# Decode state updates of a hybrid decoder step, head by head in 32- and 64-column tiles of the array

## The chip, the cores and the metric

The kernel runs on one core of one Trainium2 chip. The metric is the device time of one execution in microseconds; before the change it is 2575.82 us, the median of 3 runs (2574.97 to 2575.86).

## The reference

One inference step of a two-layer decoder trunk: 1024 prompt tokens and 8 decode sequences of 4 new tokens each (32 rows), model width 1024. Each layer projects x, runs a retention group (4 heads, keys of 32, values of 64), an HGRN2 group (4 heads, keys and values of 64) and a sliding-window attention group, joins them in one output projection, and ends with a feed-forward block; both halves end with a residual addition and a layer norm. The part that the change touches is the update of the recurrent states of the 8 decode sequences, over chunks of L = 4 tokens:

```python
# retention, per sequence n and head h: (32 keys) x (64 values)
kdec = k * jnp.exp((L - 1.0 - idx)[:, None] * lg[None, :])[None, :, :, None]
s = jnp.exp(L * lg)[None, :, None, None] * s0 + jnp.einsum('nshk,nshv->nhkv', kdec, v)
# HGRN2, per sequence and head: (64 keys) x (64 values)
bl = b[:, -1]
s = jnp.exp(bl)[..., None] * s0 + jnp.einsum('nshk,nshv->nhkv', k * jnp.exp(bl[:, None] - b), v)
```

Only products of a head's keys with the same head's values are part of the states. The outputs are the two token streams, the new states and the window caches.

## The kernel before, in words

TensorE (PE), VectorE (DVE), ScalarE (ACT), GpSimd (POOL) and the DMA queue of SyncE (SP) each run a program written out by hand, in order; `Steps` counts named events on a semaphore, and `wait_ge(S.sem, S.at(name, n))` waits for one. A layer has four stages: `project` (input projection of the first tiles), `mix` (the three head groups, tile by tile, with units of the late input projection and of the output projection in between, placed by the table `PLACES`), `attend_out` (the rest of the output projection with residual and norm) and `feed`.

`mix` goes through steps 0 to 9; in each, tile `f` is in its front part and the tile before it, `h`, in its heads part. Tiles 0 to 7 are the prompt, tile 8 the 32 decode rows. Step 9 has no dense unit; it holds only the heads part of the decode tile. There PE runs, in this order: transposes and level products, `decode_heads_out` with the partial outputs of all sequences from the old states (L1644, L1651), the **retention state products** (L1657), the joined output (L1661, L1664, L1668); then `decode_states` with the **HGRN2 state products** (L1678), and the transposes of the merged heads (L1351 from `heads_transposed`). An fp32 product is two instructions of PE in the trace.

The state products work on whole rows of the array. The 8 retention products take `kdm[0:32, b, :]`, the keys of all four heads with the rows of other sequences set to zero by POOL (L3487), as 32 x 128 weights and stream 256 value columns, so all 16 pairs of head and head come out, in banks 4 to 7; only the four diagonal ones are used. The 16 HGRN2 products take `ksm` (made by POOL, L3492) as 32 x 128 weights and stream 128 value columns, two heads at a time, again into banks 4 to 7, half of it used. PE waits before the first on `out_free` (banks 6 and 7 are shared with output units) and before the second on DVE's step "hm".

DVE adds them: `decode_states_r` (L2908) with one instruction for each retention head, 32 partitions x 512, steps "r0" to "r3", then L2911 multiplies the HGRN2 state by its decay (step "hm"). Later in the step come the normalisation of the merged heads (L2864 to L2882), `heads_low` (L2956), and `decode_states_h` (L2921), one instruction for each HGRN2 head, 64 x 512, steps "h0" to "h3".

SP waits for "h3" (L1214), stores both states (L1215, L1218), passes the barrier (L1221) and then issues the loads of `attend_out`: the norm's parameters, pieces of the output weights, the residual inputs `xin`. In `attend_out` PE's second unit writes bank 4 and waits for "h1", and the transposes of `back(l, 0, 0)`, in banks 6 and 7, wait for "h3".

Of the kernel before, what the change touches and what calls it, by code (L numbers as in the profile page):

```python
# [13 lines left out]
ALU = mybir.AluOpType  # L14
# [3 lines left out]
P = 128  # L18
DM = 1024
KT = DM // P  # L20
DEPTH = 2
SEQ = 1024
NB, NL = 8, 4
# [21 lines left out]
RV, HI = 0, 256  # L45
# [17 lines left out]
LG = [float(np.log1p(-(2.0 ** (-5.0 - h)))) for h in range(4)]  # L63
# [3 lines left out]
_at = 0  # L67
for _name, _w in (("ident", 128), ("sel", 2), ("band", 128), ("smask", 320), ("dec", 512), ("decs", 128),
                  ("inter", 128), ("inters", 128), ("kdec", 4), ("kdecs", 4), ("run", 1), ("runs", 128),
                  ("bm", 256), ("tb", 8), ("hmask", 4), ("sum4", 32)):  # L70
    CONST[_name] = (_at, _w)
    _at += _w
NCONST = _at
# [2 lines left out]
def shape_constants():  # L76

    p = np.arange(P)
    t = np.arange(P)
    c = np.zeros((P, NCONST), np.float32)  # L80

    def put(name, value):
        a, w = CONST[name]
        c[:, a:a + w] = np.asarray(value, np.float64).reshape(P, w)

    put("ident", np.eye(P))
    put("sel", p[:, None] // 64 == np.arange(2)[None])
    put("band", np.where(t[None] >= p[:, None], 0.0, NEG))
    sm = np.full((P, 2, WIN + ROWS_S), NEG)
    for r in range(P):  # L90
        b, l = r // 32, r % 4
        for rt in range(2):
            sm[r, rt, l:WIN] = 0.0
            sm[r, rt, WIN + 4 * (4 * rt + b):WIN + 4 * (4 * rt + b) + l + 1] = 0.0
    put("smask", sm)
    lg = np.array(LG)
    d = t[None, None, :] - p[:, None, None]
    dec = np.where(d >= 0, np.exp(np.maximum(d, 0) * lg[None, :, None]), 0.0) * 32 ** -0.5
    put("dec", dec)
    same = (t[None, None, :] // NL == p[:, None, None] // NL) & (t[None, None, :] < ROWS_S)  # L100
    put("decs", np.where(same, dec, 0.0)[:, :, 0:ROWS_S])
    put("inter", np.exp((t[None] + 1) * lg[p // 32][:, None]))
    put("inters", np.exp((t[None] % NL + 1) * lg[p // 32][:, None]))
    put("kdec", np.exp((P - 1 - p)[:, None] * lg[None]) * 32 ** -0.5)
    put("kdecs", np.exp((NL - 1 - p % NL)[:, None] * lg[None]) * 32 ** -0.5)
    put("run", np.ones((P, 1)))
    put("runs", np.broadcast_to(t % NL != 0, (P, P)))
    put("bm", np.broadcast_to((np.arange(ROWS_S)[None] // NL == np.arange(NB)[:, None])[None], (P, NB, ROWS_S)))
    put("tb", p[:, None] // NL == np.arange(NB)[None])
    put("hmask", p[:, None] // 32 == np.arange(4)[None])  # L110
    put("sum4", p[:, None] % 32 == np.arange(32)[None])
    lev = np.zeros((P, 2, NLEV, 64), np.int32)
    for i, half in enumerate(HALVES):
        blk, off = np.divmod(np.arange(64), half)
        lo = blk * 2 * half
        m = (p[:, None] >= lo[None]) & (p[:, None] < lo[None] + half)
        lev[:, 0, i] = m
        lev[:, 1, i] = m if half < NL else 0
    swa = np.zeros((P, 3, WIN), np.float32)
    swa[:, 0] = swa[:, 2] = np.where(t[None] <= p[:, None], 0.0, NEG)  # L120
    swa[:, 1] = NEG
    pos = np.concatenate([np.arange(SEQ), np.tile(SEQ + np.arange(NL), NB)]).astype(np.float32)
    inv_r = (10000.0 ** (-np.linspace(0.0, 1.0, 16, dtype=np.float32))).astype(np.float32)
    inv_s = (500000.0 ** (-np.arange(0, 16, 2, dtype=np.float32) / 16)).astype(np.float32)
    ar = (pos[:, None] * inv_r[None]).astype(np.float32).astype(np.float64)
    as_ = (pos[:, None] * inv_s[None]).astype(np.float32).astype(np.float64)
    rope = np.concatenate([np.cos(ar), np.sin(ar), np.cos(as_), np.sin(as_)], 1).astype(np.float32)
    return c, lev, swa, rope
# [127 lines left out]
def build(nc, A):  # L256
    ctx = ExitStack()
    with ctx:
# [19 lines left out]
        def sem(name):  # L278
            return ctx.enter_context(nc.semaphore(name))
# [40 lines left out]
        def cst(name):  # L320
            a, w = CONST[name]
            return const[:, a - P:a - P + w]
# [17 lines left out]
        x0 = [place(f"x0_{t}", [P, DM], F32, M1 + 4096 * t)[0] for t in range(TILES)]  # L340
# [24 lines left out]
        s_keep, at = place("s_keep", [P, FBLOCKS, 512], F32, u0)  # L365
# [98 lines left out]
        at = D0 + 16384  # L464
# [202 lines left out]
        zp = Steps(sem("layer_pool"), "v")  # L667
        dp = Steps(sem("decode_pool"), "zh qh0 qh1 qh2 qh3 zr qr0 qr1 qr2 qr3 kd ks0 ks1")
        dpe = Steps(sem("decode_pe"), "ckT s T w o parts st_r")
        dd = Steps(sem("decode_dve"), "zx x0 x1 s mx m nm sk den rden p0 p1 T o0 o1 r0 r1 r2 r3 hm h0 h1 h2 h3")  # L670
        da = Steps(sem("decode_act"), "ck e0 e1 sk T w o0 o1 parts")
        kv_out = sem("kv_out")
        state_out = sem("state_out")
# [187 lines left out]
        def _(sp):  # L861
# [251 lines left out]
            def mix(l):  # L1113
# [94 lines left out]
                for b in range(NB):  # L1208
# [2 lines left out]
                      .then_inc(cache_out, 16)  # L1211
                    sp.dma_start(A["s_swa_v"][bass.ds(l, 1), b, WIN - NL:WIN, :], s_v[rows, 0, :])\
                      .then_inc(cache_out, 16)
                sp.wait_ge(dd.sem, dd.at("h3", l))  # L1214
                sp.dma_start(A["s_state_ret"][bass.ds(l, 1)].rearrange("l b h k v -> (h k) (l b) v"), s0_r[:])\  # L1215
                  .then_inc(decode_out, 16)
                for pr in range(2):
# [131 lines left out]
        def _(pe):  # L1349
# [128 lines left out]
            def mix(l):  # L1478
# [158 lines left out]
                def decode_heads_out(c):  # L1637
# [14 lines left out]
                                                        start=(b < 4), stop=(b >= 4))  # L1652
                    last.then_inc(dpe.step("parts"), 1)
                    pe.wait_ge(dp.sem, dp.at("kd", l))
                    pe.wait_ge(out_free, 24 * l + KT)
                    for b in range(NB):
                        last = nc.tensor.matmul(ps[:, 4 + b // 2, (b % 2) * 256:(b % 2) * 256 + 256], kdm[0:rows, b, :],  # L1657
                                                x[0:rows, RV:RV + 256], start=True, stop=True)
                    last.then_inc(dpe.step("st_r"), 1)
                    pe.wait_ge(da.sem, da.at("parts", l))  # L1660
                    nc.tensor.matmul(ps[0:rows, 0, :], cst("sum4"), parts[:], start=True, stop=False)  # L1661
# [10 lines left out]
                def decode_states(c):  # L1672
                    x, rows = hv[c.p], c.rows
                    pe.wait_ge(dp.sem, dp.at("ks1", l))
                    pe.wait_ge(dd.sem, dd.at("hm", l))
                    for pr in range(2):
                        for b in range(NB):
                            last = nc.tensor.matmul(ps[:, 4 + 2 * pr + b // 4, (b % 4) * P:(b % 4) * P + P],  # L1678
                                                    ksm[0:rows, pr, b, :], x[0:rows, HI + pr * P:HI + (pr + 1) * P],
                                                    start=True, stop=True)  # L1680
                    last.then_inc(mpe.step("st"), 1)

                def window_weights(c, h, wave):
# [133 lines left out]
            def attend_out(l):  # L1817

                pe.wait_ge(cd.sem, cd.at("lo", TILES * l + CHUNKS))
                for j in range(KT):  # L1820
                    for half in range(2):
                        if j == 0 and half:
                            pe.wait_ge(dd.sem, dd.at("h1", l))
                        out_unit(l, KT + j, KT + 2 * j + half, slice(512 + 272 * half, 784 + 272 * half))
                        if j == 0 and half:
                            pe.wait_ge(dd.sem, dd.at("h3", l))
                            back(l, 0, 0)
                    if 1 <= j < 5:
                        again(l, 0, j - 1)
                    if j < 3:  # L1830
                        back(l, 0, j + 1)
# [721 lines left out]
        def _(dve):  # L2553
# [129 lines left out]
            def mix(l):  # L2683
# [218 lines left out]
                def decode_states_r(c):  # L2902

                    dve.wait_ge(dpe.sem, dpe.at("st_r", l))
                    for h in range(4):
                        d, e = slice(32 * h, 32 * h + 32), slice(64 * h, 64 * h + 64)
                        add = ps[d, 4:8, :].rearrange("p b (e c) -> p (b e) c", e=2)[:, :, e]
                        v.scalar_tensor_tensor(out=s0_r[d], in0=s0_r[d], scalar=float(np.exp(NL * LG[h])),  # L2908
                                               in1=add, op0=ALU.mult, op1=ALU.add).then_inc(dd.step(f"r{h}"), 1)
                    last_b = g_eb[c.p][:, :, 0:ROWS_S].rearrange("p a (b l) -> p a b l", b=NB)[:, :, :, NL - 1:NL]  # L2910
                    v.tensor_tensor(s0_h[:], s0_h[:], last_b.broadcast_to([P, 2, NB, 64]), ALU.mult)\  # L2911
                        .then_inc(dd.step("hm"), 1)

                def decode_states_h(c):
                    dve.wait_ge(dd.sem, dd.at("hm", l))
                    dve.wait_ge(mpe.sem, mpe.at("st", c.n))
                    for h in range(4):
                        pr, j = h // 2, h % 2
                        d = slice(64 * j, 64 * j + 64)
                        add = ps[d, 4 + 2 * pr:6 + 2 * pr, :].rearrange("p b (e c) -> p (b e) c", e=4)[:, :, d]  # L2920
                        v.tensor_tensor(s0_h[d, pr], s0_h[d, pr], add, ALU.add)\  # L2921
                            .then_inc(dd.step(f"h{h}"), 1)

                def decode_probs(c):
                    dve.wait_ge(da.sem, da.at("sk", l))
# [696 lines left out]
```

## Time and profile before

| | |
|---|---|
| median of 3 runs | 2575.82 us |
| profiled execution | 2577.79 us |
| its span in the trace | 2576.0 us |
| granted TensorE clock, mean | 0.979 |
| PE busy | 2448.3 us (95%), 18662 matmul instructions |
| DVE / ACT / POOL busy | 1633.6 / 983.6 / 1100.7 us |

The profile is of one execution. PE is the engine that bounds it, and the granted clock is given as a share of the full 2.4 GHz. "Idle before" in a row is the time in which the engine did nothing ahead of the instruction, with what released it. Short instructions of PE overlap, so that the rate is read from the start of one group to the start of the next.

### The profile page before, as it was taken

The page shows a single profiled execution, that of the slowest core. Times are in us where ns is not written, and L with a number is a line of the kernel's source. Part 1 is how long each engine was busy: PE and PEld are TensorE (multiplying, and loading weights), DVE is VectorE, ACT ScalarE, POOL GpSimd, SP SyncE. Part 2 cuts the span into 40 slices and gives each one's busy share as a digit, 9 for nine tenths or more (in the row PEclk, how much of TensorE's full clock was granted, in tenths as well). Part 3 has the DMA queues.
Part 4 walks back from the last instruction along what each step waited for, and adds up shares of the span by engine and source line. Part 5 has one row for each costly group of instructions (what it writes and reads, how often), then busy time and mean ns, then how long its engine had stood idle before and what let it go on. Part 6 is the DMA issues. An engine that isn't in the chain of part 4 may idle for free. (4 is left out here: it accounts for less than half of the span.)

```text
span 2576.0 us, 45626 instructions
## 1 busy us (share of the span) xinstructions
PE 2448.3 (95%) x18662; PEld 2325.6 (90%) x18662; DVE 1633.6 (63%) x2568; ACT 983.6 (38%) x1779; POOL 1100.7 (43%) x1014
## 2 busy tenths in 40 slices
PE   8999988899999999999999999888999999999997
PEld 8998876688999999999999987666889999999997
DVE  3126778546856567878741377785388555677786
ACT  3236556433322223334332456562442222333342
POOL 0027757621455553444100377674315555443440
PEclk9999999889999999999999999997999999999998
DMA  5443223162233377567533432321722333865864
GB/s 186 151 158 97 93 74 93 52 186 101 76 109 101 100 241 274 198 249 271 189 133 133 161 110 77 94 77 44 217 79 76 108 116 111 316 214 184 296 229 142
DMA packets 290880, 381.06 MB, mean 148 GB/s; under 512 B 29296, under 2 KB 206768, under 8 KB 290640
## 3 DMA queue, kind: packets, MB, share of 16 engines
q1 hardware_dynamic: 290672, 378.14, 44.5%
q8 instruction: 148, 2.42, 0.4%
q14 instruction: 60, 0.49, 0.1%
HBM read 302.46 MB, written 77.66 MB: 148 GB/s over the span
## 5 line engine op out<-in xcount | busy, mean ns | idle before, releaser
L1355 PE MATMUL ps<-hid_hi,wd_hi 128*128 128x272 f32 (+1 forms) x1536 | 439.3, 286 | 6.1 <-DVE hid_lo L3178 6.0
L1357 PE MATMUL ps<-hid_hi,wd_lo 128*128 128x272 f32 (+1 forms) x1536 | 439.2, 286 | 0.0
L1356 PE MATMUL ps<-hid_lo,wd_hi 128*128 128x272 f32 (+1 forms) x1536 | 438.6, 286 | 0.0
L1355 PEld LDWEIGHTS ps<-hid_hi,wd_hi 128*128 128x128 f32 x1536 | 291.1, 189 | 6.8 <-issue 6.8
L1357 PEld LDWEIGHTS ps<-hid_hi,wd_lo 128*128 128x128 f32 x1536 | 291.1, 190 | 0.0
L1356 PEld LDWEIGHTS ps<-hid_lo,wd_hi 128*128 128x128 f32 x1536 | 290.5, 189 | 0.0
L3561 POOL TENSOR_TENSOR wd_lo<-wd_raw,wd_hi 128x2048 fp32r<-128x2048 f32 x38 | 182.8, 4814 | 236.6 <-ACT wd_hi L2374 236.4
L3555 POOL TENSOR_TENSOR wq_lo_S<-ws,wq_hi_S 128x512 fp32r<-128x512 f32 x104 | 194.3, 1877 | 116.2 <-ACT wq_hi_S L2437 116.2
L3533 POOL TENSOR_TENSOR wl_lo<-wl_raw,wl_hi 128x2048 fp32r<-128x2048 f32 x14 | 66.1, 4721 | 382.8 <-ACT wl_hi L2105 382.8
L1356 PE MATMUL ps<-wi_lo,u_hi 128*128 128x320 f32 x600 | 185.5, 309 | 0.0
L1357 PE MATMUL ps<-wi_hi,u_lo 128*128 128x320 f32 x600 | 184.8, 308 | 0.0
L1355 PE MATMUL ps<-wi_hi,u_hi 128*128 128x320 f32 x600 | 184.5, 307 | 0.0
L1355 PE MATMUL ps<-wl_hi,u_hi 128*128 128x256 f32 (+1 forms) x640 | 182.2, 285 | 1.1 <-ACTq L693 1.1
L1356 PE MATMUL ps<-wl_lo,u_hi 128*128 128x256 f32 (+1 forms) x640 | 180.0, 281 | 0.0
L3178 DVE TENSOR_TENSOR hid_lo<-hid_raw,hid_hi 128x2112 fp32r<-128x2112 f32 x32 | 128.3, 4013 | 81.0 <-ACT hid_hi L2386 81.0
L1355 PE MATMUL ps<-t_hi_T,wq_hi_S 128*128 128x256 f32 (+1 forms) x624 | 177.7, 285 | 1.7 <-issue 1.7
L1357 PE MATMUL ps<-wl_hi,u_lo 128*128 128x256 f32 (+1 forms) x640 | 178.8, 279 | 0.0
L1356 PE MATMUL ps<-t_lo_T,wq_hi_S 128*128 128x256 f32 (+1 forms) x624 | 178.3, 286 | 0.0
L1357 PE MATMUL ps<-t_hi_T,wq_lo_S 128*128 128x256 f32 (+1 forms) x624 | 177.4, 284 | 0.0
L3555 POOL TENSOR_TENSOR wq_lo_W<-wq_raw,wq_hi_W 128x512 fp32r<-128x512 f32 x78 | 104.2, 1335 | 142.8 <-ACT wq_hi_W L2437 142.8
L2374 ACT CAST wd_hi<-wd_raw 128x2048 fp32r<-128x2048 f32 x38 | 72.6, 1911 | 211.1 <-DMA wd_raw<-in_w_down 84.6
L2648 DVE TENSOR_TENSOR wi_lo<-wi_raw,wi_hi 128x2560 fp32r<-128x2560 f32 x14 | 39.5, 2825 | 152.6 <-ACT wi_hi L2086 152.6
(373 smaller groups left out, 7610.9 us busy)
## 6 DMA issues: line engine op xcount, KB each, us to landing
wd_raw<-in_w_down SPq DMA_DIRECT2D x54, 1024.0 KB, 5.4
hid_raw<-hidscr SPq DMA_DIRECT2D x48, 1056.0 KB, 7.7
wq_raw<-in_w_up SPq DMA_DIRECT2D x26, 1024.0 KB, 5.9
wl_raw<-in_w_in SPq DMA_DIRECT2D x20, 1024.0 KB, 5.1
wi_raw<-in_w_in SPq DMA_DIRECT2D x15, 1280.0 KB, 6.4
hidscr<-h SPq DMA_DIRECT2D x32, 544.0 KB, 8.0
t_keep<-hidscr SPq DMA_DIRECT2D x16, 1056.0 KB, 12.3
hidscr<-h SPq DMA_DIRECT2D x32, 512.0 KB, 7.0
```

Source lines behind the costliest of these rows:

```text
L1355: nc.tensor.matmul(out, a_hi, b_hi, start=start, stop=False, skip_group_check=shared)
L1356: nc.tensor.matmul(out, a_hi, b_lo, start=False, stop=False, skip_group_check=shared)
L1357: return nc.tensor.matmul(out, a_lo, b_hi, start=False, stop=stop, skip_group_check=shared)
L2374: copy(wd_part("hi", j), src).then_inc(wd_hi_done, 1)
L2648: v.tensor_tensor(wi_lo[q][:], wi_raw[:], wi_hi[q][:], ALU.subtract).then_inc(wi_lo_done, 1)
L3178: v.tensor_tensor(hid_lo[j][:], src, hid_hi[j][:], ALU.subtract).then_inc(hid_lo_done, 1)
L3533: g_.tensor_tensor(wl_lo[G % 2][:], wl_raw[G % 2][:], wl_hi[G % 2][:], ALU.subtract)\
L3555: g_.tensor_tensor(wq_lo[m][:], w_quarter(m), wq_hi[m][:], ALU.subtract).then_inc(wq_lo_done, 1)
L3561: g_.tensor_tensor(wd_part("lo", j), src, wd_part("hi", j), ALU.subtract).then_inc(wd_lo_done, 1)
```

## The change

It computes each head's states with a product of its own. Retention: 32 products, weights 32 x 32 (one head's keys), 64 columns (its values), output in that head's 32 partitions of bank 4 alone. HGRN2: 32 products, weights 32 x 64, 64 columns, output in 64 partitions of bank 4 or 5. DVE adds all retention heads with one instruction over 128 x 512, its decay factor now a constant column `past4`, and all HGRN2 heads with one over 128 x 1024. The four steps "r0" to "r3" become "r" and "h0" to "h3" become "h". PE's wait on `out_free` is gone; its wait ahead of the HGRN2 states is for "r" instead of "hm"; SP's is for "h".

```diff
-                  ("bm", 256), ("tb", 8), ("hmask", 4), ("sum4", 32)):
+                  ("bm", 256), ("tb", 8), ("hmask", 4), ("sum4", 32), ("past4", 1)):
...
+    put("past4", np.exp(NL * lg[p // 32][:, None]))
...
-                sp.wait_ge(dd.sem, dd.at("h3", l))
+                sp.wait_ge(dd.sem, dd.at("h", l))
...
                     pe.wait_ge(dp.sem, dp.at("kd", l))
-                    pe.wait_ge(out_free, 24 * l + KT)
                     for b in range(NB):
-                        last = nc.tensor.matmul(ps[:, 4 + b // 2, (b % 2) * 256:(b % 2) * 256 + 256], kdm[0:rows, b, :],
-                                                x[0:rows, RV:RV + 256], start=True, stop=True)
+                        for h in range(4):
+                            d = slice(32 * h, 32 * h + 32)
+                            last = nc.tensor.matmul(ps[d, 4, 64 * b:64 * b + 64], kdm[0:rows, b, d],
+                                                    x[0:rows, RV + 64 * h:RV + 64 * h + 64], start=True, stop=True)
                     last.then_inc(dpe.step("st_r"), 1)
...
                     pe.wait_ge(dp.sem, dp.at("ks1", l))
-                    pe.wait_ge(dd.sem, dd.at("hm", l))
+                    pe.wait_ge(dd.sem, dd.at("r", l))
                     for pr in range(2):
                         for b in range(NB):
-                            last = nc.tensor.matmul(ps[:, 4 + 2 * pr + b // 4, (b % 4) * P:(b % 4) * P + P],
-                                                    ksm[0:rows, pr, b, :], x[0:rows, HI + pr * P:HI + (pr + 1) * P],
-                                                    start=True, stop=True)
+                            for j in range(2):
+                                d, at = slice(64 * j, 64 * j + 64), HI + pr * P + 64 * j
+                                last = nc.tensor.matmul(ps[d, 4 + pr, 64 * b:64 * b + 64], ksm[0:rows, pr, b, d],
+                                                        x[0:rows, at:at + 64], start=True, stop=True)
...
                         if j == 0 and half:
-                            pe.wait_ge(dd.sem, dd.at("h1", l))
+                            pe.wait_ge(dd.sem, dd.at("h", l))
                         out_unit(l, KT + j, KT + 2 * j + half, slice(512 + 272 * half, 784 + 272 * half))
                         if j == 0 and half:
-                            pe.wait_ge(dd.sem, dd.at("h3", l))
                             back(l, 0, 0)
...
-                    for h in range(4):
-                        d, e = slice(32 * h, 32 * h + 32), slice(64 * h, 64 * h + 64)
-                        add = ps[d, 4:8, :].rearrange("p b (e c) -> p (b e) c", e=2)[:, :, e]
-                        v.scalar_tensor_tensor(out=s0_r[d], in0=s0_r[d], scalar=float(np.exp(NL * LG[h])),
-                                               in1=add, op0=ALU.mult, op1=ALU.add).then_inc(dd.step(f"r{h}"), 1)
+                    v.scalar_tensor_tensor(out=s0_r[:], in0=s0_r[:], scalar=cst("past4"),
+                                           in1=ps[:, 4, :].rearrange("p (b c) -> p b c", b=NB),
+                                           op0=ALU.mult, op1=ALU.add).then_inc(dd.step("r"), 1)
...
-                    for h in range(4):
-                        pr, j = h // 2, h % 2
-                        d = slice(64 * j, 64 * j + 64)
-                        add = ps[d, 4 + 2 * pr:6 + 2 * pr, :].rearrange("p b (e c) -> p (b e) c", e=4)[:, :, d]
-                        v.tensor_tensor(s0_h[d, pr], s0_h[d, pr], add, ALU.add)\
-                            .then_inc(dd.step(f"h{h}"), 1)
+                    v.tensor_tensor(s0_h[:], s0_h[:], ps[:, 4:6, :].rearrange("p a (b c) -> p a b c", b=NB), ALU.add)\
+                        .then_inc(dd.step("h"), 1)
```

## Rows read from the trace of the kernel before

**Rows 1.** The page, part 4: shares of the chain that ended last.

```profile
PE 26%; DVE 2%; DMA 1%; issue 1%; ACT 1%; SPq 0%; DVEq 0%
```

**Rows 2.** Chain in order of time, layer 1 stretch; start us, us, what.

```profile
1784.85 4.18 PE ps L1657 x16
...
1793.29 7.16 PE ps L1678 x32
...
1801.37 0.67 DVE s_h L2921
...
1804.22 0.39 SPq L1215
...
1810.25 9.59 DMA xin<-out_y
```

**Rows 3.** Timeline of layer 0, 504 to 532: start us, us, engine, line, operation.

```profile
504.50 3.74 POOL L3492 TENSOR_TENSOR ksm<-g_kt,const 32x1024 f32<-32x1024 f32 x2
...
505.62 1.94 PE L1644 MATMUL ps<-s_r,qm_r 128*32 128x64 f32 x64 [2.02 <-DVEq L689]
...
507.30 1.96 PE L1651 MATMUL ps<-s_h,qm_h 128*32 128x64 f32 x64
...
509.20 7.19 PE L1657 MATMUL ps<-hv,kdm 32*128 32x256 f32 x16
...
516.32 1.92 PE L1661 MATMUL ps<-parts,const 128*32 128x512 f32 x2
516.42 2.83 DVE L2908 SCALAR_TENSOR_TENSOR s_r<-s_r,ps 32x512 f32<-32x512 f32 x4 [11.22 <-PE ps L1657]
...
518.16 1.06 PE L1664 MATMUL ps<-hv,r_a 32*32 32x64 f32 x8
...
519.02 1.06 PE L1668 MATMUL ps<-hv,hg_a 32*32 32x64 f32 x8
...
520.11 0.59 ACT L2202 ACTIVATE rms_sq<-ps 32x512 f32<-32x512 f32 x1 [10.20 <-PE ps L1668]
...
520.66 7.16 PE L1678 MATMUL ps<-hv,ksm 32*128 32x128 f32 x32 [0.58 <-DVE s_h L2911]
...
523.63 0.68 DVE L2882 TENSOR_TENSOR cat_h<-ps,gate 32x512 f32<-32x512 f32 x1
527.41 0.65 PEld L1351 LDWEIGHTS ps<-ident,cat_h 32*128 32x128 f32 x4
...
528.74 2.82 DVE L2921 TENSOR_TENSOR s_h<-s_h,ps 64x512 f32<-64x512 f32 x4
```

**Rows 4.** Timeline of layer 0 at 495 us: small products of the decode window.

```profile
495.04 0.65 PE L1729 MATMUL ps<-s_v,spN 32*32 32x128 f32 x8
...
495.62 0.66 PE L1726 MATMUL ps<-cv,spT 128*32 128x128 f32 x8
```

**Rows 5.** Timelines at 463 us (full clock) and at 500 us.

```profile
462.85 1.94 PE L1706 MATMUL ps<-probT,s_v 128*64 128x512 f32 x8 [1.16 <-ACT probT L2230]
...
500.63 0.98 PEld L1530 LDWEIGHTS ps<-const,g_p 128*128 128x128 f32 x4
...
501.48 1.83 PEld L1543 LDWEIGHTS ps<-lev_r,lev_x 128*128 128x128 f32 x8
```

**Rows 6.** Stages: us, busy (PE PEld DVE ACT POOL), PEclk, DMA share, GB/s.

```profile
509.20:516.32 7.12, 7.12 (x21) 5.14 (x17) 0.00 (x0) 0.58 (x1) 1.35 (x1) 0.50 0.00 0
...
528.88:531.53 2.65, 2.65 (x11) 2.65 (x12) 2.56 (x4) 0.00 (x0) 0.00 (x0) 0.50 0.00 0
...
1784.78:1787.90 3.12, 3.12 (x21) 2.70 (x15) 0.00 (x0) 0.58 (x1) 1.64 (x1) 0.99 0.00 0
```

**Rows 7.** Timeline at 551 us: a DVE addition from PSUM of the new size.

```profile
551.72 1.23 DVE L2631 TENSOR_TENSOR u_lo<-ps,u_hi 128x1024 fp32r<-128x1024 f32 x1 [0.27 <-ACT u_hi L2068]
```

**Rows 8.** Waits from 500 to 640 us: us in total, times, longest.

```profile
DVE xin L2600 <- DMA xin<-in_x: 4.1, 2, 3.0
...
PE ps L1351 <- DVE xin L2600: 3.9, 3, 1.7
```

More of the change, by code:

```diff
@@ L669, in build @@
         dpe = Steps(sem("decode_pe"), "ckT s T w o parts st_r")
-        dd = Steps(sem("decode_dve"), "zx x0 x1 s mx m nm sk den rden p0 p1 T o0 o1 r0 r1 r2 r3 hm h0 h1 h2 h3")
+        dd = Steps(sem("decode_dve"), "zx x0 x1 s mx m nm sk den rden p0 p1 T o0 o1 r hm h")
         da = Steps(sem("decode_act"), "ck e0 e1 sk T w o0 o1 parts")
```

## Prediction, made before the changed kernel ran

> **What bounds the kernel now.** I read the page's shares of the chain first, then the chain in order of time, then the timeline and the stage table of the decode stretch. The kernel is bound by TensorE (PE): most of the chain's traced share is PE, and none of the 24 products of a layer that the change rewrites costs much of a 2576 us span [rows 1]. What matters is where they stand. Each layer has one stretch, at about 505 to 531 us and 1781 to 1805 us, in which nearly nothing else can run: the last tile's decode work, after all dense units of the stage. In layer 1 the chain of waits names both groups of products in turn, L1657 (4.18 us) and L1678 (7.16 us), then the state addition of VectorE (DVE, L2921), the store that SP issues after it (L1215), and the loads queued behind that, up to the one of the next norm's input, 9.59 us with its flight [rows 2]. So every microsecond taken out of this stretch moves all that follows, if the next stage starts by the same events.
>
> The layer 0 timeline gives the order [rows 3]. PE runs the partial outputs (L1644, L1651), the retention states L1657 from 509.20 to 516.32, the joined output L1661, L1664 and L1668 to 520.08, then, after 0.58 us of waiting on DVE, the HGRN2 states L1678 from 520.66 to 527.41, then the transposes of the merged heads. Beside it runs a side chain: the output's end at 520.08 releases ScalarE (L2202), and the normalisation ends in DVE's L2882 at 523.63 + 0.68 = 524.31. The transposes need both; today PE's own queue is later by 3.1 us. After them DVE adds the states, 2.82 us, and only then SP goes on.
>
> **PE, retention states.** Before: 8 products, 16 instructions of 256 columns, 7.12 us in layer 0, that is 0.445 each at the granted clock of 0.50, the 1.2 GHz level [rows 6]. In layer 1 they take 4.18 [rows 2], since there the clock stands at the 2.4 GHz level for the first 3 us [rows 6]. After: 32 products, so 64 instructions, weights 32 x 32, 64 columns. A 64-column instruction that has its column group to itself costs 0.86 / 8 = 0.107 us from start to start (L1664 to L1668, weights 32 x 32 from the same 32 rows, clock 0.50) [rows 3]. Products that go round four column groups overlap: L1644 has 64 instructions of 64 columns in 1.68 us, L1651 has them in 1.90 [rows 3], and L1729, with 32 rows of weights as in the change, has 8 instructions of 128 columns in 0.58 us, where 8 x 0.213 = 1.7 would be due in single file [rows 4]. The new loop puts h innermost, so it goes round the four groups as well. 64 x 0.107 / 4 = 1.71 us, with 0.1 for the change of form 1.8 us. The bounds at this clock are 1.7 (L1644) and 6.9 (no overlap). I take 1.8: L1729 has the same rows and groups. Saved in layer 0: 7.12 - 1.8 = 5.3 us.
>
> **PE, HGRN2 states.** Before: 32 instructions in 6.75 us, 0.211 each [rows 3]. After: 64, weights 32 x 64, 64 columns, j innermost, two column groups in turn. The nearest row is L1706, 128 x 64 weights in two groups: 8 instructions of 512 columns in 1.94 us at full clock, where 8 x 0.427 = 3.4 would be due in single file, so two run at once [rows 5]. 64 x 0.107 / 2 = 3.4 us. The low bound is 1.8 (as if four ran at once), the high one 6.9 (none overlaps); 3.4 is nearest to L1706. That loads keep pace is less sure here. A load of 128 columns takes about 0.85 / 4 = 0.213 us at clock 0.50 (L1530, from its start to that of L1543) [rows 5], so 64 columns take 0.107 and 64 loads in single file would take 6.8 us. Yet L1644's 64 loads of 32 columns should take 64 x 0.053 = 3.4 in single file and pass in 1.7 [rows 3], so loads to different column groups overlap too.
>
> A rule speaks against this. The row first: L1664's instructions share rows and column group, and 0.107 is just their 64 columns, so a load of 0.053 hides behind the product before it [rows 3]. The Trainium skill ("TensorE: Matmul & The Clock Gate", Part 3: Packing small matmuls) says that a weight load overlaps products in flight only where the row group differs; all new products sit in the one row group 0 to 31. By that rule the loads come on top, which is the slower rival below; by the row they don't. The trace disagrees with it so far.
>
> **Waits.** The states' products now wait for DVE's "r", not "hm", and for POOL's ksm (done at 508.24) [rows 3]. "r" becomes one addition over 128 x 512 instead of four of 32 x 512; DVE's time goes by columns, 2.83 / 4 = 0.7 us [rows 3], so it ends near 511.8, before PE has done the output (514.8). The 0.58 us wait goes. The wait on out_free also goes: before L1657 no wait of note stands (L1651 runs up to it), so nothing. In the next stage bank 4's unit and the transposes now wait for the whole of "h", one addition over 128 x 1024. The same size from PSUM takes 1.23 us (L2631) [rows 7], against 2.82 [rows 3]: 1.6 saved, and done some 3 us before the unit that asks. One more constant column costs nothing I can see.
>
> **Layer 0, the sum.** Retention products end at 509.20 + 1.8 = 511.0. The output takes its 520.08 - 516.32 = 3.76: 514.8. The states' products then run to about 518.1. The side chain keeps its 524.31 - 520.08 = 4.23 us and ends at 519.0. So what is late next is no longer PE but this side chain: of 3.4 + 0.6 us saved in the HGRN2 states only about 3 count. Transposes at 519.1 instead of 527.41: 8.3 us. For DVE and SP, 1.6 more: 9.9 us.
>
> **Layer 1, the sum.** The retention products start at 1784.85. If the clock stays at 2.4 GHz until 1787.9 as now [rows 6], they take between 0.9 (half of 1.7) and 1.7, and I take 1.6, since no row shows such short instructions follow each other faster than L1644's; the output takes about half of 3.76: its end is 1788.3 and the transposes come at 1792.6, against 1793.29 + 6.75 = 1800.04: 7.4 us. If it falls at once: 1784.85 + 1.8 + 3.76 + 4.3 = 1794.7, 5.3 us. I take 6.9; with DVE's 1.6, 8.5 us.
>
> **What arrives at the end.** PE's own path gains 8.3 + 6.9 = 15.2, SP's 9.9 + 8.5 = 18.4. The next stage is led by both: PE waits three times there for the residual addition L2600, 3.9 us in all, and L2600 waits 4.1 us for its input loads [rows 8], which SP issues. When these come 1.6 us sooner, PE's waits shrink by it. The other side: dense units begin at clock 0.50 for 2.65 us [rows 6], and after a shorter, sparser stretch this may last longer; twice as long costs 1.3 us a layer, part of it under those same waits. Behind that stage PE is nearly never idle, so the shift carries to the end. I take 17.5 us, bounds 13 and 21.
>
> The profiled execution took 2577.79 us, its span of 2576.0 and 1.8 around it; it would come to 2560.3. It lies 2.0 over the median of 2575.82, so I forecast 2575.82 - 17.5 = **2558.3 us**.
>
> **Rivals.**
> *Half the overlap.* Loads go in single file, products in parallel. At clock 0.50 the retention products take 64 x 0.053 = 3.4 and the HGRN2 ones 6.8. Layer 0: output end 516.4, states' end 523.2, transposes 4.2 us earlier, SP 5.8. Layer 1: output end about 1788.4, states' end 1795.2, 4.8 and 6.4. Together 9 to 12, say 11: 2565 us. For it: the 0.213 us load; against it: L1644.
> *No overlap, loads hidden.* Then there are as many columns in single file as before: 6.9 and 6.9 us. Left are the waited 0.58 us and DVE's 1.6 a layer, about 4 in all: 2572 us, within what counts as the same. Against it: L1729, L1644, L1706.
> *Slower: loads on top.* The array loads weights of rows 0 to 31 only while no product runs in them. Each instruction then costs 0.107 + 0.053 = 0.160 (retention) and 0.107 + 0.107 = 0.213 (HGRN2) at clock 0.50: 10.2 and 13.6 us. Layer 0: +3.1 and +6.3 (the 0.58 wait gone) less 1.6; layer 1 about the same. Together +15 to +19: 2593 us. It decides from a mean start to start of 14.45 / 128 = 0.113 us over a layer's new instructions, 0.125 with DVE's gain. Against it: L1664 and L1729. This is what the skill's rule, named above, would give.
> *Given back.* The stretch shrinks as forecast but the next stage is held by its transfers, whose flight does not move with SP, and returns half: 2567 us. Against it: the transfers are issued only after the stretch.
>
> **Chances.** Forecast 0.70, half overlap 0.14, given back 0.06, no overlap 0.05, slower 0.05. The range runs from 21 us gained, 2555, to just beyond half overlap, 2566.5. A measurement of this kernel tells about 0.2% (5 us) from no change. Faster 0.90, same 0.05, slower 0.05.
>
> **What the next profile would show.** The retention products: 64 instructions a layer in 1.6 to 1.9 us; HGRN2 products: 64 in about 3.4 us, ending before DVE's merge (L2882), with an idle PE of about 1 us before the transposes. One DVE addition of 0.7 and one of 1.25 us. Stores of the states 9.9 us earlier in layer 0, 7 to 9 in layer 1. A start to start of 0.05 for 32-wide or 0.11 for 64-wide weights means half overlap; 0.16 and 0.21 the slower rival. If the stretch shrinks and the span doesn't, the shift was given back; if the clock in layer 1 differs there, its sum is off by 2 us.

## The result, and the profile after

| | before | after |
|---|---|---|
| median of the runs taken together | 2575.84 us (2574.97 to 2580.08, 4 runs) | 2556.85 us (2555.32 to 2563.2, 4 runs) |
| ratio | | 0.9909, 95% interval 0.9889 to 0.993 |
| profiled execution, its span | 2577.79, 2576.0 us | 2555.54, 2553.7 us |
| granted clock, mean | 0.979 | 0.983 |

Faster, and by the ratio more so than forecast. The forecast was 2558.3 us, 17.5 less than before, range 2555.0 to 2566.5. The two medians are 19.0 us apart, and the median after lies inside the range. The ratio puts the time at 0.9909 x 2575.84 = 2552.4 us, 23.4 less than before and 2.6 below the range; its interval, 2547.2 to 2557.8 us, reaches into the range. Later runs on other chips gave 0.9911 (0.989 to 0.9931) and 0.9908 (0.9891 to 0.9925), so the ratio repeats. The two profiles differ by 22.3 us.

The layer 0 stretch after the change, from its timeline (start us, us, engine, line, operation, idle before). It answers [rows 3].

```profile
505.03 1.93 PE L1645 MATMUL ps<-s_r,qm_r 128*32 128x64 f32 x64 [2.01 <-DVEq L690]
...
506.71 1.53 PE L1652 MATMUL ps<-s_h,qm_h 128*32 128x64 f32 x46
...
508.64 0.80 PE L1652 MATMUL ps<-s_h,qm_h 128*32 128x64 f32 x18 [0.40 <-issue]
...
509.36 1.10 PE L1659 MATMUL ps<-hv,kdm 32*32 32x64 f32 x64
...
510.39 1.04 PE L1663 MATMUL ps<-parts,const 128*32 128x512 f32 x2
510.53 0.75 DVE L2907 SCALAR_TENSOR_TENSOR s_r<-s_r,const,ps 128x512 f32<-128x512 f32 x1 [5.92 <-PE ps L1659]
...
512.37 2.08 PE L1682 MATMUL ps<-hv,ksm 32*64 32x64 f32 x64
...
516.49 0.63 PE L1352 MATMUL ps<-ident,cat_h 32*128 32x32 f32 x4 [2.04 <-DVE cat_h L2884]
...
517.66 1.21 DVE L2917 TENSOR_TENSOR s_h<-s_h,ps 128x1024 f32<-128x1024 f32 x1
...
518.90 0.39 SPq L1216 DMA_DIRECT2D out_s_state_ret<-s_r  x1
```

The 64 retention instructions pass in 510.39 - 509.36 = 1.03 us instead of 7.12, the HGRN2 ones in about 1.9 instead of 6.75. PE then idles 2.04 us for the normalisation (L2884), which now sets the end, as forecast (the idle time was forecast at about 1 us). From the first partial output to the store of the states (call it the stretch) it is 518.90 - 505.03 = 13.87 us, against 531.59 - 505.62 = 25.97 before. The stages of it (us, busy PE PEld DVE ACT POOL, PEclk, DMA share, GB/s) answer [rows 6]:

```profile
505.03:506.71 1.68, 1.68 (x65) 1.68 (x68) 0.00 (x0) 0.00 (x0) 1.68 (x2) 0.50 0.07 15
...
509.36:510.39 1.03, 1.03 (x66) 0.94 (x65) 0.00 (x0) 0.58 (x1) 0.61 (x1) 1.00 0.06 16
510.39:511.36 0.97, 0.97 (x9) 0.14 (x2) 0.83 (x2) 0.00 (x0) 0.00 (x0) 1.00 0.00 0
...
512.37:514.50 2.13, 2.08 (x66) 1.94 (x64) 0.90 (x4) 1.00 (x3) 0.00 (x0) 1.00 0.04 8
```

This is what was not foreseen: the granted clock is 1.00, the 2.4 GHz level, from the retention products to the end of the HGRN2 products, where the forecast had 1.2 GHz in layer 0. It rose at the end of the partial outputs; at their start it was 0.50. In layer 1 the stretch goes from 1771.86 to 1785.02, 13.16 us instead of 22.73. The two stretches save 12.1 + 9.6 = 21.7 of the 22.3 us of span.

### The profile page after: what moved, and what is told of

Read it like the earlier page. It is cut to its first block and busy times, and to the rows that moved or that the text cites. A ratio compares the mean times of both kernels' runs of the same rounds, so it can differ in the third digit from the quotient of the medians.

```text
span 2553.7 us, 45931 instructions
## 1 busy us (share of the span) xinstructions
PE 2429.6 (95%) x18822; PEld 2311.2 (91%) x18822; DVE 1622.3 (64%) x2556; ACT 983.1 (38%) x1779; POOL 1095.9 (43%) x1014
```

## The experiments

Two theories for the surplus. *Clock:* the products overlap as forecast, and the surplus comes from the 2.4 GHz level, which the packed work lets stand. *Chance of the place:* the clock would have been high there anyway. Beside them stood the overlap itself, which three of the forecast's four rivals deny in whole or in part, and the question whose path starts the next stage.

All readings of the stretch are collected here; each comes from the timeline of one profile. "Output" is the time from the joined output's first instruction to the first HGRN2 product: 1.98 us at 2.4 GHz, 3.69 at 1.2. In the kernels with the old additions it also holds the wait for DVE after it: 3.7 and 0.58 us at 1.2 GHz make the 4.34 of before, and so 4.33 can hide a fast output. In layer 1 of before_p4 and of warm_before it is 2.05 us at 2.4 GHz and a wait of 2.29.

| kernel | layer 0: stretch, retention, output | layer 1 |
|---|---|---|
| before | 25.97, 7.12, 4.34 | 22.73, 4.17, 4.34 |
| before_again | 22.75, 4.39, 4.34 | 22.73, 4.10, 4.34 |
| before_p2 | 22.76, 4.40, 4.34 | 22.75, 4.26, 4.34 |
| before_p3 | 25.96, 7.13, 4.33 | 22.72, 3.90, 4.34 |
| before_p4 | 23.30, 3.89, 4.34 | 20.48, 3.65, 4.33 |
| after | 13.87, 1.03, 1.98 | 13.16, 1.08, 1.98 |
| after_again | 13.60, 1.02, 1.98 | 16.50, 1.86, 3.69 |
| after_third | 13.39, 1.40, 1.98 | 16.02, 1.86, 3.69 |
| after_p4 | 13.27, 1.19, 1.98 | 13.04, 1.03, 1.98 |
| h_only | 21.15, 7.12, 3.68 | 20.91, 7.12, 3.69 |
| r_only | 15.49, 1.03, 2.17 | 15.01, 1.37, 2.17 |
| in_row | 21.28, 5.70, 3.69 | 18.48, 3.11, 3.47 |
| four_adds | 17.75, 1.86, 3.69 | 14.88, 1.08, 1.98 |
| early_add | 11.97, 1.03, 1.98 | 12.16, 1.39, 1.98 |
| early_again | 14.52, 1.86, 3.69 | 12.47, 1.02, 1.98 |
| early_warm | 10.32, 1.02, 1.98 | 10.44, 1.03, 1.98 |
| warm_before | 22.93, 3.86, 4.33 | 20.50, 3.65, 4.34 |
| warm_after | 13.48, 1.03, 1.98 | 11.81, 1.03, 1.98 |

**after_again: the changed kernel once more.**

> The changed kernel once more, to see whether the TensorE clock in the two decode stretches is a property of the change. Theory 'clock follows the work': its state products and the output after them run at the 2.4 GHz level again in both layers (about 1.0 us for the 64 retention instructions, 1.9 for the HGRN2 ones), 21 to 23 us less than before. Rival 'chance of the place': in at least one layer the clock is at 1.2 GHz for part of the stretch (1.8 and 3.4 us), and the gain is 15 to 19 us.

Ratio 0.9911. Layer 0 ran as in the first profile, layer 1 at 1.2 GHz. Its timeline there:

```profile
1776.27 1.93 PE L1659 MATMUL ps<-hv,kdm 32*32 32x64 f32 x64
...
1778.13 1.92 PE L1663 MATMUL ps<-parts,const 128*32 128x512 f32 x2
...
1781.82 3.68 PE L1682 MATMUL ps<-hv,ksm 32*64 32x64 f32 x64
...
1785.94 0.63 PE L1352 MATMUL ps<-ident,cat_h 32*128 32x32 f32 x4 [0.44 <-DVE cat_h L2884]
```

Start to start the retention products take 1.86 us (forecast 1.8), the output 3.69 (3.76), the HGRN2 products about 3.4 (3.4). So at 1.2 GHz the sum's prices hold to a tenth. The stretch is 16.50 - 13.16 = 3.3 us longer than layer 1 of the first profile. Of this 2.5 us are the clock (0.78 in the retention products, 1.71 in the output; beyond them the normalisation sets the end at either level), and 0.85 us are a gap in the partial outputs, described at the end. The span is 2559.1 us, 16.9 less than before. That is near the forecast's size, but by luck: the forecast had stretches of 16.1 and 14.2 us, and they took 13.60 and 16.50.

**in_row: same products, no turns between column groups.**

```diff
-                        for b in range(NB):
-                            for h in range(4):
+                        for h in range(4):
+                            for b in range(NB):
...
-                            for j in range(2):
+                        for j in range(2):
```

> The changed kernel with the loops turned: all eight sequences of one head in a row, so consecutive products stay in the same 32- or 64-column group; same products, same sizes, same additions. Theory 'groups overlap': the 64 retention instructions go in single file, 64 x 0.053 = 3.4 us at the 2.4 GHz level (6.8 at 1.2), instead of 1.03, the HGRN2 ones 3.4 instead of 1.9, of which about 2 us are hidden beside the normalisation: 2.4 to 3 us a layer, 5 to 6 us slower than the change in all; up to 14 if the clock falls to 1.2 GHz. Rival 'it is the smaller work, not the overlap': durations and time as in the change within 2 us.

Median 2567.72 us, ratio 0.9944 (0.9926 to 0.9962), beside 0.9911 for the change on the same chip: about 8.5 us worse.

```profile
509.87 5.77 PE L1659 MATMUL ps<-hv,kdm 32*32 32x64 f32 x64
...
519.26 5.98 PE L1682 MATMUL ps<-hv,ksm 32*64 32x64 f32 x64
...
515.57:519.26 3.69, 3.69 (x20) 1.85 (x19) 1.88 (x2) 0.00 (x0) 0.00 (x0) 0.50 0.00 0
...
1780.96:1784.07 3.11, 3.11 (x69) 3.02 (x65) 0.00 (x0) 0.59 (x1) 1.37 (x1) 1.00 0.00 0
```

Layer 0 stands at 1.2 GHz (0.50): 5.70 us in single file against 1.86 packed at that clock. Layer 1 has the 2.4 GHz level for just the retention products: 3.11 against 1.03. Both are a factor of 3.0. For the two-group products it is 5.91 (519.26 to the transposes at 525.17, with no idle time) against about 3.4, 1.7. So the order alone, at equal clock, gives the overlap; the rival "no overlap" falls, and so do "half the overlap" and "loads on top". Single file is somewhat cheaper than my 0.107 us an instruction: 0.089.

**r_only and h_only: half of the change each.** r_only is the old kernel with the retention part of the diff, `past4` and one addition, the wait on `out_free` kept; h_only has the HGRN2 part, one addition, and the wait for "r3" in place of "hm".

> The kernel before with only the retention half of the change (32 x 32 tiles, one bank, one DVE addition). Theory 'clock follows the work': with the old 7.1 us of sparse wide products gone, the clock stays at 2.4 GHz through the output: layer 0 saves 6 + 1.8 us and layer 1 about 3 + 1.8, and the old HGRN2 products take 3.4 to 6.8 us: 12 to 18 us less than before. Rival 'clock is not moved by it': layer 0 saves 5.3 us, layer 1 2.5 us, and 0.6 each for the wait on DVE: 9 us less.

> The kernel before with only the HGRN2 half (32 x 64 tiles, two banks, one DVE addition at the end, the wait on hm gone). The old retention products leave the clock at 1.2 GHz, so the HGRN2 products take 3.4 us; the normalisation chain of 4.2 us then sets the end: 3.1 us a layer less on TensorE, 1.6 more by the single addition: 8 to 10 us less than before. By the rival in which PE's own path and not SP's sets the start of the next stage, 6 us.

r_only: median 2561.36, ratio 0.9919 (0.9898 to 0.9939), 21 us, above the upper expectation. h_only: 2573.08, 0.996 (0.9944 to 0.9976), 10 us. The halves add up to more than the whole, 31 us against 23, and their stretches do so too (15.9 and 4.4 us less than the mean of before, against 18.2). The table shows why the first is so strong: in both layers the clock is at 2.4 GHz through output and old HGRN2 products, 3.93 us to the transposes instead of 6.96. In h_only, with the old retention products ahead, it is at 1.2 throughout (7.12 us in both layers). So in these two runs the high clock came with the retention half. How far that half is its cause two profiles cannot say: the old retention products ran at 1.2 GHz from start to end in only two of the ten stretches of before.

**warm_before and warm_after: clock raised by hand.** Both get five extra products ahead of the waits of `heads_out`; their result is not used.

```diff
+                    if not c.prompt:
+                        for _ in range(5):
+                            nc.tensor.matmul(ps[:, 2, 0:P], ident, ident, start=True, stop=True)
```

> The kernel before with the same five extra products. If a warm start were enough, the old stretch would run at 2.4 GHz to its end: retention products 3.4 us, output 1.9, HGRN2 products 3.4, about 8 us less in layer 0 and 5 in layer 1: 12 to 16 us less than before, most of what the change brought. If the clock is held up only by packed work, it falls again during the old wide products, as it did in layer 1 of the kernel before: 0 to 4 us less than before.

> The changed kernel with five extra 128 x 128 fp32 products of the identity (10 instructions, result unused, bank 2) put in front of the partial outputs, into the 2 us in which TensorE waits there for VectorE. Theory 'the clock sets the rest': with the engine busy there the clock comes to the 2.4 GHz level before or during the partial outputs in both layers and in every run, which then take about 1.1 + 1.1 us instead of 1.7 + 1.9; 1 to 3 us less than the change, and less spread between runs. Rival 'clock is not moved': the extra products cost 0 to 0.5 us a layer and nothing else changes.

warm_before: ratio 0.9975 (0.9962 to 0.9989), 6 us. Layer 1 of it:

```profile
1785.86:1789.51 3.65, 3.65 (x25) 2.88 (x17) 0.00 (x0) 0.59 (x1) 2.34 (x2) 1.00 0.00 0
...
1793.85:1799.83 5.98, 5.98 (x32) 5.98 (x33) 2.41 (x7) 0.42 (x2) 0.00 (x0) 0.59 0.01 3
```

Here the old retention products and the output (2.05 us) do run at 2.4 GHz, and then PE waits 2.29 us for DVE's four old additions and "hm" (L2914), and the clock falls early in the HGRN2 products (mean 0.59). In layer 0 it falls with the retention products. So a warm start is not enough for the old work: it comes to 6 of the 23 us, and its two stretches take 43.4 us against 46.4 in before. warm_after: ratio 0.9904 (0.9887 to 0.992), no clear difference from the change. Three of its four groups of partial outputs took 0.89 to 1.27 us instead of 1.7 and 1.9, but in the fourth PE paused 1.72 us without a releaser. The profiled execution is the slowest of its six runs, 2566.8 us against a median of 2557.25; its two stretches take only 25.3 us, so that lies elsewhere.

**four_adds and early_add: whose path starts the next stage.** four_adds splits the addition of L2917 back into four, with the same products and banks; early_add moves `decode_states_h(h)` ahead of `heads_low(h)`.

> The changed kernel with its single HGRN2 addition split back into four of 64 x 512 (same banks and products). If the start of the next stage follows SyncE's loads, which wait for this addition: 1.6 us a layer, 3.2 us slower than the change. If it follows TensorE's own path: 0 to 0.5 us slower. Between the two if each leads for a part.

> The changed kernel with VectorE's single HGRN2 addition moved one place forward, ahead of the small low-part subtraction (L2952), into the time in which VectorE waits for the transposes and ScalarE. SyncE gets its event about 1.2 us earlier a layer, TensorE's first dense unit starts about 0.2 us later. If SyncE's loads set the next stage: 1.5 to 2.4 us less than the change; if TensorE's path does: 0 to 0.5 us more.

four_adds: median 2564.32, ratio 0.9928 (0.9915 to 0.9941), by the ratios some 4 us worse than the change; its layer 0 also had the low clock. early_add: 2555.61, 0.9897 (0.9883 to 0.9912), 3 us better by the middle, within the intervals. The place where it shows is the next stage, in layer 0. There the lag is the time from the transposes to SP's store, and the next stage is reached at its first up-projection product (`wu_hi`).

| layer 0 | lag | store to `wu_hi` | transposes to `wu_hi` |
|---|---|---|---|
| five profiles of before | 4.0 | 61.7 to 61.9 | 65.7 to 65.9 |
| four_adds | 4.0 | 61.6 | 65.6 |
| four profiles of after | 2.3 to 2.4 | 61.5 to 62.5 | 63.9 to 64.9 |
| early_add, early_again, early_warm | 1.1, 1.3, 1.1 | 63.0, 63.8, 62.7 | 64.1, 65.0, 63.8 |

From a lag of 4.0 to one of 2.4 the first distance stays and the second falls by most of the 1.6 us: SP's loads lead. From 2.4 to 1.1 it is the other way: the first distance grows by about 1 us and the second hardly moves, so of the 1.3 us that the earlier addition brings little is left. r_only, with a lag of 4.0 and 63.1 us, fits neither, and in layer 1 the distances scatter by 2 us, too much to read.

**after_third, early_again, early_warm, before_again, on one chip.** early_warm is early_add plus the five products.

> The changed kernel a third time, beside early_add on the same chip. Two of its four stretches seen with packed products were at 2.4 GHz in both layers, one fell to 1.2 in layer 1. Theory 'packed work usually lifts the clock, where it stands decides the rest': stretch from the first partial output to the store of the states 13.2 to 13.9 us in a layer at 2.4 GHz, 16.5 at 1.2 GHz, nothing between except a change on the way; 17 to 24 us less than before.

> The changed kernel with the HGRN2 addition one place earlier, again, beside the changed kernel. SyncE's event leads the next stage (the distance from it to the next stage's first up-projection product was 62.3 us in kernels where it follows TensorE's transposes by 4.0 us, and 62.2 where by 2.4), so 1.2 us a layer, 2.4 us less than the change; 0 if TensorE's path leads as soon as the distance is under 2.4 us.

> early_add with the five extra products ahead of the partial outputs. If a raised clock in the partial outputs is worth its 1.5 us a layer: 2 to 3 us less than early_add. If, as the one before suggests, a pause of TensorE without a releaser inside them (0.4 to 1.7 us) takes it back: within 1 us of early_add.

> The kernel before, profiled once more. Theory 'only packed work holds the clock': the retention products, the output and the HGRN2 products stand at 1.2 GHz in both layers, save up to 3 us of the retention products after the partial outputs; stretch of 22 to 26 us. Rival 'chance of the place': in one layer the whole stretch is at 2.4 GHz, about 16 us.

Ratios: after_third 0.9908 (0.9891 to 0.9925), early_again 0.9899 (0.9883 to 0.9915), early_warm **0.988** (0.9864 to 0.9896), median 2551.38, its four runs within 2550.38 to 2552.92. So the early addition alone is not told from the change. With the warm start the kernel is about 7 us faster than the change; the intervals just overlap, but each of its four runs is below every run of the change (2554.06 at least) and of early_again (2555.39) on the same chip. Layer 0 of early_warm:

```profile
504.72 1.18 PE L1648 MATMUL ps<-s_r,qm_r 128*32 128x64 f32 x64
...
506.72 1.10 PE L1662 MATMUL ps<-hv,kdm 32*32 32x64 f32 x64
...
515.04 0.39 SPq L1216 DMA_DIRECT2D out_s_state_ret<-s_r  x1
```

From the partial outputs to the HGRN2 products the clock is at 2.4 GHz in both layers (0.89 in the first group of layer 0, 1.00 in the others): stretches of 10.32 and 10.44 us. My expectation of "within 1 us of early_add" from the pause was wrong: no pause came. before_again speaks against the chance theory: its output and HGRN2 products are at 1.2 GHz in both layers. One of the profiles that follow speaks for it.

**before_p2, before_p3, before_p4, after_p4: what is left.**

> The kernel before, profiled once more: its two profiles so far lie at 2578 us, the low end of its runs (2574 to 2589). If slower executions are those in which the decode stretches stand at 1.2 GHz throughout, both stretches take 26 us and the span is 3 to 6 us longer. If the stretches take 23 to 26 us as before and the span is longer all the same, the rest of the spread lies outside what the change touches.

> The kernel before, profiled once more, with the same question as the one ahead of it: stretches of 26 us in both layers if the clock there makes the slow executions, 23 to 26 us with a longer span if it does not.

> The kernel before, profiled once more, with the same question: stretches of 26 us in both layers if the clock there makes the slow executions, 23 to 26 us with a longer span if it does not.

> The changed kernel, profiled a fourth time: each stretch 13.2 to 13.9 us if its clock is at 2.4 GHz from the retention products on, 16.5 if at 1.2.

In layer 1 of before_p4 the old kernel, with nothing added, kept the clock through its wide retention products and the output, and PE waited for DVE as in warm_before:

```profile
1785.93:1789.58 3.65, 3.65 (x24) 2.89 (x17) 0.00 (x0) 0.58 (x1) 1.96 (x1) 1.00 0.00 0
1789.58:1791.62 2.04, 2.04 (x19) 1.05 (x18) 1.87 (x3) 0.00 (x0) 0.00 (x0) 1.00 0.00 0
...
1793.91 5.74 PE L1678 MATMUL ps<-hv,ksm 32*128 32x128 f32 x32 [2.29 <-DVE s_h L2911]
```

So what the chance theory asks for does occur, once in the ten stretches of before.

Spans 2578.4, 2580.4, 2573.9 and 2554.6. Over the five profiles of before the two stretches take 43.8 to 48.7 us, 46.4 on average; over the four of after 26.3 to 30.1, 28.2 on average: 18.2 us saved there. The mean spans are 2577.1 and 2556.6, 20.5 apart. The time outside the stretches runs from 2527.3 to 2532.9 in before and from 2526.7 to 2529.5 in after. The longest profile of before, 2580.4, has long stretches (48.7, 2.3 above the mean) and a rest 1.1 above the mean; but the first profile has the same stretches and a span of 2576.0. So both parts make the spread. 2.3 us of the mean gain lie in the rest too, which with five and four profiles is not told from chance.

The runs give 23 us and the profiles 20.5, which is inside the interval of the first ratio (18 to 29 us). Yet the difference has one direction. In each of the kernels tried, the gain by the ratio is 3.5 to 7.8 us more than what its stretches save against the mean of before. The runs of before on the later chips have medians of 2582 to 2582.5 us, its five profiled executions a mean of 2578.9. So some 3 us may lie in executions of before that no profile shows. What makes them longer stays open.

## Why the prediction was right and wrong

*The place.* Right as far as the profiles show: 21.7 of 22.3 us lie in the two stretches in the first pair and 18.2 of 20.5 on average, and the following stages kept it. "Given back" did not happen.

*The overlap, and the rivals to it.* Right, by in_row: factors of 3.0 and 1.7 at equal clock, and 1.86 and 3.4 us at 1.2 GHz where 1.8 and 3.4 were forecast. The weights of one row group do load while products of other column groups run. The rule of the Trainium skill ("TensorE: Matmul & The Clock Gate", Part 3: Packing small matmuls), that a load overlaps only where the row group differs, does not hold in these traces: with all weights in rows 0 to 31, loads were busy for 0.94 us of the 1.03 in which the retention products passed.

*What is late next.* Right, for the kernel with both halves: the normalisation, with PE idle 2.04 us at 2.4 GHz (0.44 at 1.2), and DVE's additions of 0.75 and 1.21 us (forecast 0.7 and 1.23).

*The clock.* This step failed. The layer 0 sum took every duration at 1.2 GHz, because [rows 6] showed 0.50 there, and priced the output at its old 3.76 us. But the clock in a row belongs to the work that stood there. The two terms that were off: the output, 3.76 forecast and 2.05 measured (510.39 to 512.44), and the retention products, 1.8 and 1.03. That is 2.5 us, and 0.45 more come from a side chain 0.25 shorter than priced and from the transposes' start, read at the load (527.41) and not at the product (527.62). Against it stand 0.75 us by which the partial outputs were longer, with PE's pause in them: layer 0's surplus of 12.1 - 9.9 = 2.2. In layer 1 I had taken 6.9 between 5.3 and 7.4, and 9.6 came for 8.5. There the retention term was wrong even for a high clock: 1.6 was taken because no row showed faster issue than L1644, but L1644 ran at 0.50; it measured 1.08.

How the clock differs shows over all profiles. In both kernels it rose at the same place, in the partial outputs or up to 0.6 us into the retention products, so the kernels differ in when it fell. Over 16 stretches with packed retention products and no extra ones (the four profiles of after, early_add, early_again, four_adds, r_only) it rose in 12 and stood at 2.4 GHz through the output in all 12; in 4 it stayed at 1.2. Over 14 with wide or single-file products (five profiles of before, h_only, in_row) it rose in 9 and fell again before the output's end in 8; in the ninth, layer 1 of before_p4, it stood through the output. Whether the packing itself holds it, or that the output follows so soon, is not separated, and what decides whether it rises at all is not known.

*Luck in the first profile.* The forecast was built on the profile of before with the longest stretches of the five, 48.7 us against 46.4 on average, which made the saving 2.3 us too large. The clock made it about 2.1 us too small: the stretches of after take 28.2 on average, where the sum for SP's path had 30.3. The two errors nearly cancel. So the clock accounts for the surplus of the first pair of profiles, 21.7 against 18.4, but not for all of the ratio's 23.4: what lies beyond the stretches stays open, as said above.

*SP before PE.* The forecast set PE's gain at 15.2 and SP's at 18.4 and took 17.5 between them. SP's path leads down to a lag of about 2.4 us (four_adds against after; early_add shows that it does not below). Had I followed it, the sum would have been 18.4, near the 18.2 that the stretches save on average, by the luck just told.

*The range.* Its lower end, 21 us of gain, stands without a working, and no bound for the clock in layer 0 is named. With the output and the products at 2.4 GHz there, 2.5 us more, the low end would have been 2552.5, about where the ratio lies.

## What to carry to other kernels

Where the array is fed small products, turn their order so that neighbours fall into different column groups: the same instructions took a third of the time with four groups and 0.6 of it with two, even with all weights in one row group. When work in a low-clock stretch is made denser, price what follows it at both clock levels, for the clock that a row shows is the old work's. And read which event starts the next stage: here it was SyncE's loads behind a VectorE addition, not TensorE's own path, and what shortened that addition counted, until the other path was level with it. Last, one profile is one draw: the old kernel's stretches took 43.8 to 48.7 us over five.

## What the runs showed of the hardware that was not expected

- 64 fp32 instructions of 64 columns in four column groups passed in 1.03 us at 2.4 GHz, 16 ns from start to start. The Trainium skill ("TensorE: Matmul & The Clock Gate", Back-to-back issue gap) has an issue floor of about 25 ns for up to 64 columns; these traces, with the column group changing each time, have less.
- With the packed products TensorE's clock, once up, stood at 2.4 GHz through the output in 12 of 12 stretches (from 509.36 to 514.50 in the first profile). Inside or right behind the wide or single-file products it fell in 8 of 9 (mean 0.87 over the 4.17 us of layer 1 before, 0.50 behind them).
- PE paused inside the partial outputs with no releaser in the trace in several kernels, the old one too: 0.40 us in after, 0.47 in layer 1 of after_again, 1.72 in warm_after, 1.44 in warm_before, 0.16 in before_p4. From start to start the first two cost 0.75 and 0.85 us. early_warm and the first profile of before had none. What it is was not tried.
